# Attention heads signalled one by one, and two output copies moved ahead of the widest exponentials

## What is computed

```python
for l in range(DEPTH):                       # DEPTH = 2
    ...
    s = einsum('bqhd,bkhd->bhqk', q_blk, k) * scale      # 128 queries of one head
    s = where(causal, s, -inf)                           # D adds a bias, C a choice of 128 keys a query
    p = softmax(s, axis=-1)
    o = einsum('bhqk,bkhd->bqhd', p, v)
    ...
    x = x + mixed @ w_out[l]
```

## Time and profile before

| | |
|---|---|
| median of 3 runs | 1834.51 us (1832.82 to 1835.68) |
| the profiled execution | 1833.93 us, of which the span is 1832.0 us |
| PE busy | 1787.4 us, 98% of the span |
| DVE, ACT, POOL busy | 51%, 36%, 40% |
| granted TensorE clock, mean | 0.996 of full |
| PE in the chain that ended last | 89% |

### The profile page before, as it was taken

One profiled execution on the slowest core, in us unless ns is written; L12 is line 12 of the kernel. 1 busy time (PEld: TensorE's weight loads), 2 busy tenths in 40 slices (PEclk: granted clock), 3 DMA queues, 4 the chain that ended last, 5 costly groups with the idle time before them and its releaser, 6 DMA issues.

```text
span 1832.0 us, 22979 instructions
## 1 busy us (share of the span) xinstructions
PE 1787.4 (98%) x9057; PEld 1458.8 (80%) x9057; DVE 929.6 (51%) x1508; ACT 660.2 (36%) x1230; POOL 727.8 (40%) x328
## 2 busy tenths in 40 slices
PE   9999899999999999998999999999999999999997
PEld 8677668888888886776688888888788988888786
DVE  4678752514232246797627372727522134339374
ACT  4543553312222235345523121222535343442212
POOL 4232434444444533333344444544343334334442
PEclk9999999999999999999999999999999999999999
DMA  7225002222232232210025424243242223113211
GB/s 233 70 69 172 2 24 92 93 92 92 93 112 93 68 96 99 69 70 1 24 69 187 182 92 161 92 168 98 83 149 69 92 70 138 57 64 104 77 69 46
DMA packets 104448, 171.00 MB, mean 93 GB/s; under 512 B 21616, under 2 KB 39432, under 8 KB 103209
## 3 DMA queue, kind: packets, MB, share of 16 engines
q1 hardware_dynamic: 103320, 169.79, 27.8%
q10 hardware_dynamic: 1040, 0.00, 0.0%
HBM read 166.56 MB, written 7.93 MB: 95 GB/s over the span
## 4 chain that ended last, share of the span: by engine, by line
PE 89%; DVE 7%; ACT 2%; issue 1%; DMA 0%; SPq 0%; DVEq 0%; ACTq 0%
PE G L2101 26%; PE G L2103 25%; PE G L2102 25%; PE S L2388 2%; PE S L1103 1%; DVE select L1941 1%; PE G L2424 1%; DVE work L1777 1%; DVE neg_max L1977 1%; PE S L2149 1%; PE S L1077 1%; DVE top L1776 1%; PE G L2372 1%; PE S L1088 1%; PE G L2405 1%
## 5 line engine op out<-in xcount | busy, mean ns | idle before, releaser
L1332 POOL TENSOR_TENSOR w_lo<-raw,w_hi 128x1024 fp32r<-128x1024 f32 (+2 forms) x268 | 657.7, 2475 | 972.4 <-ACT w_hi L1378 665.3
L2101 PE MATMUL G<-h_hi,w_hi 128*128 128x512 f32 x896 | 355.4, 397 | 1.9 <-DVE h_lo L861 1.9
L1378 ACT ACTIVATE w_hi<-raw 128x2048 fp32r<-128x2048 f32 (+1 forms) x94 | 178.9, 1904 | 492.7 <-PE G L2103 492.7
L2103 PE MATMUL G<-h_hi,w_lo 128*128 128x512 f32 x896 | 349.3, 390 | 0.0
L2102 PE MATMUL G<-h_lo,w_hi 128*128 128x512 f32 x896 | 348.9, 389 | 0.0
L2101 PE MATMUL G<-w_hi,h_hi 128*128 128x512 f32 (+2 forms) x704 | 277.2, 394 | 2.2 <-DVE h_lo L1730 1.2
L2103 PE MATMUL G<-w_hi,h_lo 128*128 128x512 f32 (+2 forms) x704 | 267.1, 379 | 0.0
L2102 PE MATMUL G<-w_lo,h_hi 128*128 128x512 f32 (+2 forms) x704 | 266.7, 379 | 0.0
L2101 PEld LDWEIGHTS G<-h_hi,w_hi 128*128 128x128 f32 x896 | 168.2, 188 | 39.3 <-issue 4.4
L2103 PE MATMUL G<-w_hi,u_lo 128*128 128x512 f32 x512 | 199.2, 389 | 0.0
L2101 PE MATMUL G<-w_hi,u_hi 128*128 128x512 f32 x512 | 199.2, 389 | 0.0
(11 more groups left out here) (317 smaller groups left out, 2223.4 us busy)
## 6 DMA issues: line engine op xcount, KB each, us to landing
raw<-in_w_in_dram SPq DMA_DIRECT2D x40, 1024.0 KB, 5.1
raw<-in_w_up_dram SPq DMA_DIRECT2D x32, 1024.0 KB, 5.0
raw<-in_w_down_dram SPq DMA_DIRECT2D x32, 1024.0 KB, 4.9
raw<-in_w_out_dram SPq DMA_DIRECT2D x12, 1024.0 KB, 4.9
w_ada<-in_w_ada_dram SPq DMA_DIRECT2D x4, 3072.0 KB, 11.9
skew_scratch<-line_scratch SPq DMA_DIRECT2D x1, 4608.0 KB
raw<-in_w_in_dram SPq DMA_DIRECT2D x8, 512.0 KB, 4.0
raw<-in_w_in_dram SPq DMA_DIRECT2D x4, 832.0 KB, 6.6
```

The lines of the kernel that those rows point to most:

```text
L1332: ins = pool.tensor_tensor(w_lo[:, c % SPLIT_SLOTS, part, 0:n], raw[:, c % RAW_SLOTS, part, 0:n], w_hi[:, c % SPLIT_SLOTS, part, 0:n].bitc ...
L1378: act.activation(w_hi[:, c % SPLIT_SLOTS, :, 0:n], raw[:, c % RAW_SLOTS, :, 0:n], ACT.Copy).then_inc(high_ready, 1)
L2101: pe.matmul(dst, a_hi, b_hi, start=first, stop=False)
L2103: return pe.matmul(dst, a_lo, b_hi, start=False, stop=last)
```

## The change

- `exponentials`: head 0 now signals for itself (`first_summed`), head 1 as before (`score_drained`).
- `invert_sums`: two instructions of one column instead of one of two; the first waits for head 0's sum.
- `scale_probs`: two instructions, one for each head; `give_probs` waits for each head apart.
- `take_output`: in the step whose exponentials are those of a widest item, ACT copies output i - 2 too, ahead of these exponentials. Elsewhere the copies keep their places.
- `MID_HIGH`: four pieces of 512 columns at steps 4, 5, 8 and 9, where two of 1024 columns stood at steps 6 and 8. The signal to POOL comes with the last of them.

```diff
-MID_HIGH = {6: slice(0, 2), 8: slice(2, 4)}
+MID_HIGH = {4: 0, 5: 1, 8: 2, 9: 3}
...
-            def scale_probs(i, done):
-
+            def scale_probs(i, done, items):
+
+                def scaled(e):
+                    part = prob[:, i % 2, e, 0:P * len(key_tiles(i))]
+                    inverse = inv_sum[:, i % 4, e:e + 1].broadcast_to(list(part.shape))
+                    return pool.tensor_tensor(part, part, inverse, ALU.mult)
+
+                pool.wait_ge(first_inverted, items + (i + 1))
+                scaled(0).then_inc(first_scaled, 1)
                 pool.wait_ge(inv_ready, done + (NB + i + 1))
-                part = prob[:, i % 2, :, 0:P * len(key_tiles(i))]
-                inverse = inv_sum[:, i % 4, :].unsqueeze(2).broadcast_to([P, 2, part.shape[2]])
-                pool.tensor_tensor(part, part, inverse, ALU.mult).then_inc(prob_scaled, 1)
+                scaled(1).then_inc(prob_scaled, 1)
...
                     for e in range(2):
-                        ins = act.activation(prob[:, i % 2, e, 0:width], S[:, 2 * (i % 2) + e, 0:width], ACT.Exp,
-                                             bias=neg_max[:, i % 2, e:e + 1], accum_out=row_sum[:, i % 4, e:e + 1])
-                    ins.then_inc(score_drained, 1)
+                        act.activation(prob[:, i % 2, e, 0:width], S[:, 2 * (i % 2) + e, 0:width], ACT.Exp,
+                                       bias=neg_max[:, i % 2, e:e + 1], accum_out=row_sum[:, i % 4, e:e + 1]
+                                       ).then_inc(score_drained if e else first_summed, 1)
...
+                taken = 0
                 for i in range(NI + 1):
 
-                    if i > 2:
-                        take_output(i - 3)
+
+                    widest = i + 1 < NI and ITEMS[i + 1][1] == TT - 1
+                    if i > 2 and taken < i - 2:
+                        take_output(taken)
+                        taken += 1
                     take_qk(*next_qk(i))
                     if i:
                         take_probs(i - 1)
+                    if widest and i > 1:
+                        take_output(taken)
+                        taken += 1
                     if i + 1 < NI:
                         exponentials(i + 1)
...
                 def invert_sums(i):
+                    dve.wait_ge(first_summed, item0 + (i + 1))
+                    dve.reciprocal(inv_sum[:, i % 4, 0:1], row_sum[:, i % 4, 0:1]).then_inc(first_inverted, 1)
                     dve.wait_ge(score_drained, score0 + (i + 1 + PAIR_CREDIT))
-                    dve.reciprocal(inv_sum[:, i % 4, :], row_sum[:, i % 4, :]).then_inc(inv_ready, 1)
+                    dve.reciprocal(inv_sum[:, i % 4, 1:2], row_sum[:, i % 4, 1:2]).then_inc(inv_ready, 1)
...
                 def give_probs(i):
-                    pe.wait_ge(prob_scaled, item0 + (i + 1))
                     for e in range(2):
+                        pe.wait_ge(prob_scaled if e else first_scaled, item0 + (i + 1))
```

More of the change, by code:

```diff
@@ L566, in build @@
         inv_ready, prob_scaled = sem("inv_ready"), sem("prob_scaled")
+        first_summed, first_inverted, first_scaled = sem("first_summed"), sem("first_inverted"), sem("first_scaled")
         side_even, side_odd = sem("side_even"), sem("side_odd")
@@ L1354, in _ @@
                 for i in range(NI):
-                    scale_probs(i, l * LAYER_SC)
+                    scale_probs(i, l * LAYER_SC, l * NI)
                     if i in MID_LOW:
@@ L1592, in part_high @@
                     ins = act.activation(w_hi[:, c % SPLIT_SLOTS, part], raw[:, c % RAW_SLOTS, part], ACT.Copy)
-                    if part.stop == HALF_K:
+                    if part == HALF_K - 1:
                         ins.then_inc(high_ready, 1)
@@ L1617, in _ @@
                         high_mix(k)
+                assert taken == NI - 2
                 take_output(NI - 2)
```

## The result

| | before | after |
|---|---|---|
| median | 1835.1 us (1832.31 to 1841.77, 20 runs) | 1840.82 us (1835.62 to 1847.38, 20 runs) |
| profiled execution | 1833.93 us, span 1832.0 us | 1845.18 us, span 1843.4 us |
| PE busy | 1787.4 us, 98% | 1800.2 us, 98% |
| granted clock, mean of the profiled execution | 0.996 | 0.989 |

The ratio is 1.0032, with a 95% interval of 1.0022 to 1.0042: the change costs 0.3%, above the 1837.6 us at which my range ended. The profiled execution of after is one of its longer ones, 4.4 us above the median, which makes it a good one to read and a bad one to take a size from. Later comparisons each have their own median of the kernel before, measured beside them: 1834.74, 1835.83 and 1834.65 us.

A forecast was written before the change was run, and what follows sets the result against it. PE, busy 98%, was the bound, with DVE's run behind the widest items the longer way in the attention stages. Profiled 1833.93 + 0.64 (inverses) - 1.21 (old fall) + 1.2 (new fall) = 1834.56, said 1834.6 us; range 1831.5 to 1837.6.

The forecast's parts named there:

- PE's 0.75 us goes, and PE's 0.46 us at 197.92 becomes about 1.2: Output copied early, pairs 1 to 4 of both layers: PE's wait moves from the output copy to DVE, net 0.
- The second inverse: DVE behind the top rounds: eight extra inverses on the chain at 0.08 us each, +0.64 us, bounds 0 and 1.36.
- The mixT_bc waits: Last pair of each layer: at most 0.5 us a layer to gain; taken as 0, bounds 0 to -1.0 us.
- The weight pieces: Smaller weight copies on ACT: PE waits some 0.3 us for POOL at item 10, hidden by DVE; net 0.
- Rival 3: Widest items: early output copy holds up ACT's exponentials, 12 x 0.3 = +3.6 us, 1838.2 us; chance 0.04.
- Rival 1: Both attention layers: removing PE's output-copy waits is a real gain of 10.2 us, giving 1822.5 us; chance 0.05.
- The sign that I had named for being wrong: Profile after, attention stages: a clock below 0.97 would show the prediction wrong the other way.
- I take one fall, at its old price: PE's clock at the gathered idle time of four pairs: one fall, +1.2 us, bounds 0 and 6.4.
- rival 2: PE's clock falls more often: three falls instead of one, 1838.2 us; chance 0.15 for two or more, 0.06 for three.
- -1.21 us: First layer, behind item 7's 1.77 us output wait: that wait and its clock fall go, saving 1.21 us.
- The bound of 6.4 us for the clock term: Upper bound for clock falls at the gathered idle places: four falls of 1.6 us each.
- PE's list of waits has no row for POOL ... gain 0 on the path: Heads signalled apart: head 0 reaches POOL about 0.7 us sooner, but PE never waits for POOL, so gain 0.

The follow-up runs named there:

- e2_heads: The kernel before with only the heads signalled, inverted and scaled apart: 1835.34 us, ratio 1.0002.
- y1_rounds_only: The kernel before with only one of the two top rounds behind each widest item done a step earlier: 1829.87 us, ratio 0.9977.
- e1_copies: The kernel before with only the early output copies, heads kept together: 1834.79 us, ratio 1.0000.

## Why the prediction was wrong

**What held.** "PE's 0.75 us goes, and PE's 0.46 us at 197.92 becomes about 1.2" is what the timeline after shows (1.33 us), and at full clock the fourth pair keeps its length of 9.51 us: DVE's run behind the widest item was the longer way, net 0. The second inverse starts 0.07 us behind the first in this timeline of DVE after:

```profile
198.56 0.69 DVE L1985 TENSOR_SCALAR qkT<-G 96x512 f32<-96x512 f32 x1
199.16 0.15 DVE L1997 RECIPROCAL inv_sum<-row_sum 128x1 f32<-128x1 f32 x1
199.23 0.14 DVE L1999 RECIPROCAL inv_sum<-row_sum 128x1 f32<-128x1 f32 x1
199.29 0.67 DVE L1992 TENSOR_REDUCE neg_max<-S 128x2 f32<-128x512 f32 x1
```

Eight of them make an estimated 0.5 to 0.6 us. The medians of `e2_heads` and before differ by 0.6, as much as the prediction's +0.64, but that is no confirmation: the interval reaches from -1.7 to +2.0 us. The mixT_bc waits, from which I hoped for up to 1.0 us, grew instead to 1.3 us a layer; `e2_heads` alone has them at 0.9 in the first. The weight pieces brought a wait of 0.2 us for POOL at item 10 where I had 0.3. Rival 3 did not come: the early copy at item 3 ends at 193.03, and the exponentials start at 193.18, released by the maxima. Rival 1 was wrong for the reason given, and `y1_rounds_only` shows the other side of it: the output waits are worth something once a round is off DVE's way. The sign that I had named for being wrong came too: the clock in the stages is 0.94 and 0.92, below 0.97.

**The step that failed** is the last term of the sum, "I take one fall, at its old price". I had put the idle time in the right place and nearly in the right size, named the mechanism as rival 2, and gave it 0.15. The profiled execution has three falls in the stages, of some 7, 3 and 14 us at half clock, where before had one of some 3 us; so both the number and the price were too low. By the medians, with +0.64 and -1.21 us kept, the loss of 5.7 us leaves about 6.3 us for this term, where I had put 1.2. The reason that I gave against it was that 1.77 us of waiting did it only once in two. That single wait was the wrong thing to count by: the new pattern is 2.01 us of standing within 2.65 us, which the lists put into two pairs of each layer, with 1.34 us at once in another. In the profiled execution it stands three times, and half clock followed each time. The bound of 6.4 us for the clock term just held the 6.3, but my range stopped at 1837.6, because I let the small chance cut the bound off.

**The step behind it** is "PE's list of waits has no row for POOL ... gain 0 on the path". For the time of the path it is true (`e2_heads`). For the pattern of idle time it is not: the row is missing only while the output copy holds PE. With the copy moved the row appears (0.53 us in `e1_copies`), and it is this wait that keeps PE's idle time in parts. Signalling the heads apart removes it and gathers the rest. I looked at each part against the lists of before and never at one part against the lists that the other makes.

The size, at last, is a matter of how often. The Trainium skill (TensorE: Matmul & The Clock Gate, Part 1, "A second HAM failure mode: psum-queue depth-cycling") tells of a kernel in which short idle times between groups of matmuls come often enough for the clock to swing between its two levels. The trace shows such a swing, with 0.50 in the windows from 202 to 208 between windows at 1.00, but behind one gathered wait rather than many short ones; here PE is 98% busy over the program. In the runs of after the mean clock is anything from 0.988 to 0.995, so no single execution has the number of falls for the kernel.

**Left open.** What makes one gathered wait bring a fall and the next not (six of seven did) was not settled, nor was why some kernels fall ahead of the stages. Nor do the runs tell whether it is the place of the standing or its amount that counts: gathered it is 2.01 us, in three parts 1.7 to 1.8. That before's fall behind item 7 happened in one layer of two, with equal waits, stays unexplained as well.

## What to carry to other kernels

Where PE is nearly always busy, ask of a change not only how long PE waits but where the waiting then lies: two microseconds of standing nearly in one place cost about 5 us of clock over the program here, and 1.7 us cut into three parts cost nothing that could be measured. Before believing that a part is neutral, set it against the lists that the other parts make. And first look for what the gathered wait is waiting for: one top round a pair, moved into the time in which DVE stood idle, turned 1840.8 into 1827.2 us.

## What the runs showed of the hardware

- Within one kernel the mean granted clock of a run tells its time to about 1 us: at one listed clock the 71 runs of before lie at most 2 us apart, and 0.001 is worth 1.4 us (1.6 us in after, from 0.988 to 0.995). Sorting runs by it tells a change of work from a change of clock where the medians cannot.
- Idle transpositions into a free bank held the clock at full: 8 at each of eight places, an estimated 1 us of PE each time by the row of 11 in 1.42 us, made 1834.9 us of 1840.8, with a mean clock of 0.9959 where it had been 0.9920.
- Waits of PE of 1.33 and 0.68 us with 0.64 us of work between them were followed by 3 to 14 us at half clock in six cases of seven, in a program in which PE is 98% busy.
- A one-column reciprocal that stands queued behind another costs DVE 0.06 to 0.07 us from start to start, with a duration of 0.14 to 0.15 in the rows.
